# A three-block float32 model: convolution sums in two PSUM banks, and a recurrence in six levels with the next head's decay chain pulled forward

## The reference

```python
h = rmsnorm(concat(meta_tokens, x), norm_g)
glu_a, glu_b, z_conv, q, f, i, g_rec, m_conv, m_rec = split(h @ w_in)     # each 1024 wide
# convolution branch: 31 taps along the tokens, each channel by itself
a = glu_a * sigmoid(glu_b)
c = causal_conv(a, conv_w[31 taps]) + conv_b
y_conv = (silu(layernorm(c)) * silu(z_conv)) @ w_conv_out
# recurrence branch: 8 heads of 128 channels, in chunks
q = silu(q);  f = lb + (1 - lb) * sigmoid(f);  k = 1 - f;  v = i
b = cumsum(log f) within a chunk
o_intra[t] = sum_{s<=t} (sum_k q[t,k] k[s,k] exp(b[t,k] - b[s,k])) v[s]
o_inter[t] = (q[t] * exp(b[t])) @ S;   S = exp(b_last) * S + (k * exp(b_last - b))^T v
o = o_inter + o_intra, normalised per head, times silu(g_rec), then @ w_rec_out
out = x + (sigmoid(m_conv) * y_conv + sigmoid(m_rec) * y_rec) @ w_out
```

## Time and profile before

| | |
|---|---|
| median of 3 runs | 4041.17 us (4039.98 to 4044.63) |
| profiled execution | 4043.46 us, span of the trace 4041.8 us, so 1.7 us lie around it |
| mean granted TensorE clock | 0.965 |
| PE busy | 3775.2 us (93%) |
| DVE busy | 1746.9 us (43%) |
| ACT busy | 1139.4 us (28%) |
| POOL busy | 1018.8 us (25%) |
| chain that ended last | PE 76%, DVE 18%, ACT 3% |

### The profile page before, as it was taken

The page is one execution under the profiler, slowest core; times in us unless marked ns, Lnnn a source line. Parts: engine busy times, 40 slices in busy tenths (PEclk is TensorE's granted clock), DMA queues, the critical chain, the costliest instruction groups (busy, mean ns, idle before and its releaser), DMA issues.

```text
span 4041.8 us, 41623 instructions
## 1 busy us (share of the span) xinstructions
PE 3775.2 (93%) x17820; PEld 3089.0 (76%) x17820; DVE 1746.9 (43%) x1962; ACT 1139.4 (28%) x1412; POOL 1018.8 (25%) x408
## 2 busy tenths in 40 slices
PE   6999999998999989999989999998999979999996
PEld 6888887877778867666778888886777758888884
DVE  4565633999952344223332222224557152222225
ACT  4454432212141233443221111113322131111112
POOL 3343331222233431001322222222112332222221
PEclk9999999999999989999989999999999989999997
DMA  2000011111132221000211111112101201111111
GB/s 97 27 27 27 27 53 60 50 42 52 66 127 94 94 90 44 31 23 25 84 41 48 47 47 42 48 48 86 32 32 42 78 26 48 47 47 42 48 48 51
DMA packets 57927, 210.97 MB, mean 52 GB/s; under 512 B 6416, under 2 KB 6544, under 8 KB 57616
## 3 DMA queue, kind: packets, MB, share of 16 engines
q1 hardware_dynamic: 57744, 208.31, 15.4%
HBM read 183.12 MB, written 25.17 MB: 52 GB/s over the span
## 4 chain that ended last, share of the span: by engine, by line
PE 76%; DVE 18%; ACT 3%; issue 2%; POOL 1%; DMA 1%; SPq 0%; DVEq 0%; ACTq 0%
PE psum L418 65%; DVE Cb L1767 8%; PE psum L499 3%; PE psum L737 2%; PE psum L723 1%; PE psum L472 1%; PE psum L457 1%; DVE hl L1607 1%; PE psum L759 1%; DVE fb L1701 0%; DVE B L2310 0%; DVE Cb L1762 0%; POOL hl L2375 0%; DVE k L2252 0%; DVE work L1712 0%
## 5 line engine op out<-in xcount | busy, mean ns | idle before, releaser
L2358 POOL TENSOR_TENSOR wl<-raw,wh 128x1024 fp32r<-128x1024 f32 x283 | 707.7, 2502 | 2538.2 <-ACT wh L979 2538.2
L418 PE MATMUL psum<-hh,wh 128*128 128x512 f32 (+2 forms) x3760 | 1173.2, 398 | 98.0 <-POOL wl L2358 41.7
L418 PE MATMUL psum<-hh,wl 128*128 128x512 f32 (+2 forms) x3760 | 1123.9, 385 | 0.0
L418 PE MATMUL psum<-hl,wh 128*128 128x512 f32 (+2 forms) x3760 | 1118.3, 383 | 0.0
L418 PEld LDWEIGHTS psum<-hh,wh 128*128 128x128 f32 x3760 | 679.9, 194 | 244.9 <-issue 89.9
L418 PEld LDWEIGHTS psum<-hh,wl 128*128 128x128 f32 x3760 | 708.3, 192 | 137.8
L418 PEld LDWEIGHTS psum<-hl,wh 128*128 128x128 f32 x3760 | 705.9, 192 | 135.0
L979 ACT ACTIVATE wh<-raw 128x1024 fp32r<-128x1024 f32 x283 | 298.4, 1054 | 834.0 <-PE psum L418 827.3
L1767 DVE SCALAR_TENSOR_TENSOR Cb<-av,vec,Cb 128x1024 f32<-128x1024 f32 x240 | 376.2, 1567 | 8.3
L2092 DVE TENSOR_TENSOR B<-B,psum 128x1024 f32<-128x1024 f32 x128 | 156.4, 1222 | 491.1 <-PE psum L418 491.1
L418 PE MATMUL psum<-hdh,wh 128*128 128x512 f32 x1024 | 324.0, 397 | 0.0
(11 more groups left out here) (362 smaller groups left out, 3050.4 us busy)
## 6 DMA issues: line engine op xcount, KB each, us to landing
raw<-in_wts SPq DMA_DIRECT2D x283, 512.0 KB, 3.5
keep_x<-B SPq DMA_DIRECT2D x16, 512.0 KB, 3.8
t<-keep_x SPq DMA_DIRECT2D x15, 512.0 KB, 3.2
X<-in_xin SPq DMA_DIRECT2D x8, 520.0 KB, 5.2
keep_sz<-tmp SPq DMA_DIRECT2D x8, 512.0 KB, 2.9
av<-keep_gr SPq DMA_DIRECT2D x8, 512.0 KB, 3.2
tmp<-keep_sz SPq DMA_DIRECT2D x8, 512.0 KB, 3.8
av<-keep_gc SPq DMA_DIRECT2D x8, 512.0 KB, 3.3
```

The costliest lines, as they stand in the source:

```text
L418: ins = pe.matmul(out, w, x[:, k, c0:c0 + width], start=first and n == 0, stop=final and n == 2)
L2358: gp.tensor_tensor(wl[:, s, :], raw[:, s, :], fp(wh[:, s, :]), SUB).then_inc(*c.lo.tick(i))
```

## The change

Two things are changed at once, both in the first block.

**Convolution.** The running sum of the taps is a PSUM tile, `taps`, on banks 6 and 7; only the last tap writes `Cb[:, m]`. So that these banks are free, the ring `aux` is cut to bank 5 for this stretch, and the second of the two `gn` spreads goes into `head`'s bank.

**Recurrence.** Levels of halves 64 to 4 stay. The two smallest (2 and 1) and the diagonal become one last level over blocks of four tokens, whose mask includes the diagonal; for it ACT takes two full-width exponentials, DVE multiplies `kb` and `qb` in place by them, and `level(LAST, kk, q)` uses these. So a head has six levels instead of eight. The chain gate, logarithm, scan, difference, exponential and "kd" product of head h+1 is issued inside head h's job, in a fifth slot of `work` called `decay`; so are the differences of its levels 0 to 3 and the multiplications of levels 0 and 1. Both banks of a level are now issued in one step, the two transposes of a kind too. For head 0 the chain is issued before the first job.

```diff
-HALVES = (64, 32, 16, 8, 4, 2, 1)
+HALVES = (64, 32, 16, 8, 4, 2)
+LAST = len(HALVES) - 1
...
-        work = sb("work", [P, 4, TM], F, s)
+        work = sb("work", [P, 5, TM], F, s)
...
+    decay = work[:, 4, :]
+    def lev(lv):
+        return work[:, lv % 4, 0:T]
+    taps = flat(psum[:, 6:8, :])
...
@@ tensor(), hgrn(h)
+            pe.wait_ge(*c.ev("v", h, 2))
+            turned_v(0)
+            turned_v(1)
+            yield
+            pe.wait_ge(*c.hg_dve("kd", h))
+            turned_k(0)
+            turned_k(1)
+            yield from pause(2)
+            level(0, lev(0), lev(0))
+            yield
...
+            level(2, lev(2), lev(2))
+            yield from pause(2)
+            state(1)
+            yield
+            level(3, lev(3), lev(3))
+            yield from pause(3)
+            level(4, lev(4), lev(4))
+            yield from pause(3)
+            level(LAST, kk, q)
+            yield from pause(3)
+            output(0)
+            yield
+            output(1)
...
@@ tensor(), convolution
+                pe.wait_ge(*c.cv_act("root", 1))
+                aux.only(psum[:, 5, :])
...
-                x = grab(aux, ("gn", m, j), c.cv_dve("og", m, j))
+                x = grab((aux, head)[j], ("gn", m, j), c.cv_dve("og", m, j))
...
@@ scalar(), hgrn(h)
+            hgrn_exps(h, 4)
+            yield from pause(2)
+            se.wait_ge(*c.hg_pool("d", h, LAST))
+            se.wait_ge(*c.hg_pe("A", h, 2, 1))
+            se.activation(lev(LAST + 1), lev(LAST), EXP, scale=-1.0).then_inc(*c.hg_act.tick("e-", h, LAST))
+            se.wait_ge(*c.hg_act("e-", h, LAST))
+            se.activation(lev(LAST), lev(LAST), EXP).then_inc(*c.hg_act.tick("e", h, LAST))
+            yield
+            if ahead:
+                hgrn_log(ahead)
+            yield from pause(2)
+            if ahead:
+                hgrn_decay(ahead)
+            yield
+            se.wait_ge(*c.hg_pe("A", h, 3, 1))
+            se.activation(lev(LAST + 2), bx, EXP).then_inc(*c.hg_act.tick("qe", h))
...
@@ vector(), hgrn(h)
+            keep(2)
+            if ahead:
+                hgrn_gate(ahead)
+            yield
+            hgrn_mults(h, 4)
+            yield
+            state(1)
+            if ahead:
+                hgrn_scan(ahead)
+            yield
+            keep(3)
+            if ahead:
+                hgrn_decay(ahead)
+            yield from pause(2)
+            if ahead:
+                hgrn_kd(ahead)
+            yield
+            keep(4)
+            ve.wait_ge(*c.hg_act("qe", h))
+            ve.tensor_tensor(qe, qe, q, MUL).then_inc(*c.hg_dve.tick("qe", h))
+            yield
+            ve.wait_ge(*c.hg_dve("qe", h))
+            ve.tensor_tensor(kx, kx, lev(LAST + 1), MUL)
+            ve.tensor_tensor(q, q, lev(LAST), MUL).then_inc(*c.hg_dve.tick("right", h, LAST))
+            yield from pause(2)
+            keep(LAST)
+            yield from pause(3)
+            if ahead:
+                hgrn_mults(ahead, 0)
...
@@ vector(), convolve(m)
-            ve.tensor_scalar(Cb[:, m, :], u[:, 0:T], V("conv_w", m), V("conv_b", m), MUL,
+            if m:
+                ve.wait_ge(*c.cv_dve("c", m - 1))
+            ve.tensor_scalar(taps, u[:, 0:T], V("conv_w", m), V("conv_b", m), MUL,
                              ADD).then_inc(*c.cv_dve.tick("tap", m, 0))
             for j in range(1, TAPS):
+                last = j == TAPS - 1
                 ve.wait_ge(*c.cv_dve("tap", m, j - 1))
-                ve.scalar_tensor_tensor(Cb[:, m, :], u[:, j:j + T], V("conv_w", 8 * j + m), Cb[:, m, :], MUL,
+                ve.scalar_tensor_tensor(Cb[:, m, :] if last else taps, u[:, j:j + T], V("conv_w", 8 * j + m), taps, MUL,
...
@@ gpsimd(), hgrn(h)
+            yield from pause(9)
+            if ahead:
+                gp.wait_ge(*c.hg_dve("scan", ahead))
+                gp.wait_ge(*c.hg_pe("A", h, 4, 1))
+                below(ahead, 0)
+            yield from pause(2)
+            if ahead:
+                gp.wait_ge(*c.hg_dve("right", h, LAST))
+                below(ahead, 1)
```

More of the change, by code:

```diff
@@ L493, in turned_v, with level @@
                 ins.then_inc(*c.hg_pe.tick("vT", h, g))
[L495 to L500, removed]
+            def level(lv, left, right):
+                pe.wait_ge(*c.hg_dve("right", h, lv))
+                for g in range(2):
+                    x = grab(aux, ("A", h, lv, g), c.hg_dve("A", h, lv, g))
+                    for n in range(4):
+                        cc = slice((4 * g + n) * 128, (4 * g + n + 1) * 128)
+                        ins = pe.matmul(x[:, n * 128:(n + 1) * 128], left[:, cc], right[:, cc], start=True, stop=True)
+                    ins.then_inc(*c.hg_pe.tick("A", h, lv, g))
             def turned_k(g):
@@ L515, in state, with output @@
                 ins.then_inc(*c.hg_pe.tick("S", h, g))
[L517 to L553, removed]
+            def output(g):
                 x = grab(aux, ("o", h, g), c.hg_act("o", h, g))
[L555 to L558, removed]
+                pe.wait_ge(*c.hg_dve("A", h, LAST, g))
                 for n in range(4):
@@ L1101, in hgrn @@
             yield
[L1102 to L1111, removed]
+            hgrn_exps(h, 4)
[11 more added lines that the diff above has]
+                hgrn_decay(ahead)
+            yield
+            se.wait_ge(*c.hg_pe("A", h, 3, 1))
+            se.activation(lev(LAST + 2), bx, EXP).then_inc(*c.hg_act.tick("qe", h))
+            yield from pause(5)
+            if ahead:
+                hgrn_exps(ahead, 0)
+            yield from pause(2)
             for g in range(2):
@@ new lines, in hgrn_kd, with hgrn_mults @@
+        def hgrn_kd(h):
+            ve.wait_ge(*c.hg_act("wd", h))
+            ve.tensor_tensor(decay, decay, kb[:, h % 2, :], MUL).then_inc(*c.hg_dve.tick("kd", h))
+        def hgrn_mults(h, lv):
+            ul, ur = half(lev(lv), HALVES[lv])
+            ve.wait_ge(*c.hg_act("e", h, lv))
+            ve.tensor_tensor(ul, ul, half(kb[:, h % 2, META:TM], HALVES[lv])[0], MUL)
+            ve.tensor_tensor(ur, ur, half(qb[:, h % 2, :], HALVES[lv])[1], MUL).then_inc(*c.hg_dve.tick("right", h, lv))
@@ new lines, in hgrn, with keep @@
+            qe = lev(LAST + 2)
+            ahead = h + 1 if h < 7 else None
+            def keep(lv):
+                m = masks[:, lv:lv + 1, :].to_broadcast([P, 4, 128])
+                for g in range(2):
+                    dst, src = chunks(Ab[:, g * 512:(g + 1) * 512], 4), chunks(aux.of("A", h, lv, g), 4)
+                    ve.wait_ge(*c.hg_pe("A", h, lv, g))
+                    if lv == 0:
+                        ve.tensor_tensor(dst, src, m, MUL).then_inc(*c.hg_dve.tick("A", h, lv, g))
+                    else:
+                        ve.wait_ge(*c.hg_dve("A", h, lv - 1, g))
+                        ve.copy_predicated(dst, m.bitcast(I32), src).then_inc(*c.hg_dve.tick("A", h, lv, g))
@@ L1689, in hgrn @@
[L1689 to L1698 removed]
+            yield from pause(4)
@@ new lines, in hgrn @@
+        def hgrn(h):
+            ahead = h + 1 if h < 7 else None
+            yield from pause(4)
+            gp.wait_ge(*c.hg_pe("A", h, 0, 1))
+            below(h, 4)
+            yield from pause(2)
+            gp.wait_ge(*c.hg_pe("A", h, 1, 1))
+            below(h, LAST)
+            yield from pause(9)
+            if ahead:
+                gp.wait_ge(*c.hg_dve("scan", ahead))
+                gp.wait_ge(*c.hg_pe("A", h, 4, 1))
+                below(ahead, 0)
+            yield from pause(2)
+            if ahead:
+                gp.wait_ge(*c.hg_dve("right", h, LAST))
+                below(ahead, 1)
+            yield from pause(3)
+            if ahead:
+                below(ahead, 2)
+            yield from pause(2)
+            if ahead:
+                gp.wait_ge(*c.hg_pe("o", h, 1))
+                below(ahead, 3)
@@ L2421, in gpsimd @@
         for h in range(8):
+            if h == 0:
+                split(HGRN + 3)
+                gp.wait_ge(*c.hg_dve("scan", 0))
+                for lv in range(4):
+                    below(0, lv)
             for n in range(3):
```

241 lines of the change are left out of this document (100 added, 141 removed).

## The result

The changed kernel takes 3968.44 us (median of 4 runs, 3966.78 to 3970.26) against 4040.57 (4 runs, 4039.64 to 4044.63): ratio 0.982, interval 0.9803 to 0.9837. The forecast was 3977, its range 3932 to 4006. The profiled execution has a span of 3967.0, 74.8 less than before.

The account below looks back on a forecast made before the run. PE, busy 93% of the span, was taken to lose time to waits, in the convolution through DVE's taps. Convolution 37, seven heads 19 and the last head 8.5 made 64.5: 4041.2 - 64.5 = 3977 us, range 3932 to 4006.

Parts of the forecast that it names:

- The convolution, 37 us: Convolution: 30.5 us between the spreads plus the last spread's wait of 5.07 and its slow clock of about 1.5.
- I expect it to stop meeting POOL: Convolution: a tap reading one SBUF and one PSUM tile is no longer stretched by POOL; 68 us of DVE time go.
- The cover: Convolution: PE's slack over DVE per channel group, 2 us (48.1 against 46); above 1.38 us a tap DVE bounds again.
- the sum by rows: Convolution taps: from profile rows, a PSUM source adds nothing; 1.29 us a tap, against the skill's 0.065 us more.
- The wait at the last level: Recurrence: PE waits about 5.5 us a head for L1774, between 1.6 and 7, behind a DVE chain of 22 us.
- the 4 to 7 that the prediction named as its sign: Recurrence: the profile after would show PE waiting for L1774 seven times, 4 to 7 us each, none at the transposes.
- The slow clock: Recurrence: PE's reduced clock behind the wait at the last level costs 2 us a head.
- PE's own work: Recurrence: PE's work a head without waits and slow clock falls from 55.5 to 51.8 us.
- issuing halves together saves a further 0.5: Recurrence, PE: 0.5 us a head saved beyond the 3.2 us of the two levels dropped.
- the handovers: Recurrence: twelve handovers take about 0.2 us off a head's gain, so 2.7 us is counted instead of 2.9.
- The rivals: Chain hidden 0.12, dearer PSUM tap 0.14, heads gain nothing 0.10, slower by PSUM taps 0.04, no measurable effect 0.04.
- rival 1: Recurrence: chain hidden, PE waits 1.6 us or less, no slow clock, heads 52.5 to 54, 3921 to 3932; chance 0.12.

Follow-up runs that it names:

- experiment 5: Changed kernel with the taps' running sum alternating between the PSUM banks and the SBUF result tile: 3976.51 us, ratio 0.9837.
- Experiment 3: Also `late_split`: changed kernel with POOL's split of one slab held back until the last level's last product (L1774) is done: 3940.72 us, ratio 0.9752.
- experiment 4: Changed kernel with the next head's scan, difference, "kd" behind the last level's products on DVE, `qe`'s exponential ahead of the next decay on ACT: 3929.82 us.

## Why the prediction was right, step by step

- **The convolution, 37 us: right, and shown.** 30.5 between the spreads and 6.5 behind them. The spreads come every 48.1, and the step "I expect it to stop meeting POOL" is shown by experiment 5. The price of a tap was 1.290 (taken 1.29), and 1.323 from tap to tap (27.78 us for 21 of them). The cover is 3.0 us a group (DVE's wait for the slab's evacuation), the forecast had 2.
- **The PSUM source.** Taps that read PSUM and write SBUF take 1.281; those of the kernel before, which read and write SBUF, 1.285 in the median. The 62 further cycles that the Trainium skill, "VectorE: DVE Perf Modes", section "The TRN2 errata", gives a PSUM source are not in these rows; the sum by rows was the right one. What experiment 5 shows agrees with the Trainium skill, "SBUF — State Buffer", section "Who interferes with whom": a DVE instruction with two SBUF inputs contends with a GpSimd instruction that reads SBUF, one with at most one SBUF input (outside the two-port modes) does not.
- **The wait at the last level: right in place and mechanism, 3.8 in place of 5.5.** The chain took 20.8 us (274.16 to 294.97), forecast 22: undisturbed 17.3 (forecast 18.0), POOL 3.5 (0.9 at the gate, 0.5 at `qe`, 2.15 at L1774; forecast 4). The gate and the last product met POOL as forecast. The difference `below(h+1, 0)` started beside "kd" as forecast, but "kd" kept its time (1.24) and `qe` behind it was the one stretched. PE had 17.1 us of its own (274.16 to 291.25), forecast 16.4. So the wait came out at 3.70 to 3.78, under the 4 to 7 that the prediction named as its sign. Experiment 3 shows the one cause, the collision, and experiment 4 against 3 the other, the place in DVE's order.
- **The slow clock: 2.1 us in six heads of seven, forecast 2.0.** After a wait of 3.70 the first head had its last level in 2.05 us, at full speed, and took 57.4; the other six took 59.5 in the mean behind nearly the same wait (3.77 or 3.78).
- **PE's own work: the term that was too low.** Taken 51.8, measured 57.39 - 3.70 - 0.66 = 53.0. One step is seen to fail: "issuing halves together saves a further 0.5". Sixteen products of a level take 1.70 (272.46 to 274.16), more than two halves of 0.81. The rest, some 0.7, is in what I took off the kernel before for its slow clock: its heads were 62.6 to 63.7 apart, so the loss differs from head to head and one head's 2.8 was too much for all. Behind head 1's wait, for instance, the clock is 0.50 only from 152.6 to 156.0 us, with 3.3 us of PE's work in it: 1.6 lost. Three heads lost 2.8, the other four 1.6 or 1.7, in the mean 2.1. PE's own work before was then 56.3 a head and not 55.5, and the 3.3 by which it fell is about what two levels cost (3.2).
- **What the moved chain itself gave: next to nothing as it stood.** Waits and slow clock together took 6.6 us a head before (62.9 less 56.3) and 6.2 after (59.2 less 53.0). So of the 25.8 us of the seven heads some 23 are the two levels that are gone. This split is worked out from the traces; no run has the levels or the moved chain alone. Experiment 4 shows what the chain was worth in another place: 38.6 us more, of which 27.7 come already when the collision alone goes (experiment 3).
- **The sum.** A head took 59.2 where 60.0 stood (60.2 with the handovers), 6.8 us less for seven; the last job took 9.4 less (12.1 less the 2.7 that come behind it) where 8.5 stood; with the 0.6 ahead of the heads, 3.6 in stages that the change does not touch, and 1.6 given back to the clock behind the heads, that is the 10.3 us by which the span shrank more than forecast (74.8 for 64.5). The medians differ from the forecast by 8.6. That a head came so close is in part luck: PE's own work was 1.2 us more than taken and the wait 1.7 less, and the two errors, 8 and 12 us over seven heads, cancel for the most part.
- **The rivals.** None of the five occurred. Experiment 3 makes the kernel much like rival 1 (waits of 1.6 us, no slow clock), yet its heads are 55.3 apart and not 52.5 to 54, since PE's own work is 53.0 and not 51.8, and it takes 3941 where rival 1 has 3921 to 3932. Experiment 4 reaches 3930 by another order of DVE's row, which moves the products out of the split's way and the chain out of theirs.

## What to carry to other kernels

A wait that vanishes is looked for again one place further on: here 28.2 us left the transposes and 26.5 came back at the last level, because a chain that nobody needed yet stood in an in-order queue ahead of one that was needed next. Order such a queue by who is waited for first. And where POOL runs beside a long running sum, try the sum in PSUM, so that DVE reads only one of its large inputs from SBUF: here POOL then cost the taps nothing.

## What the hardware showed that was not expected

- Where DVE and POOL meet, the one that comes second waits: L1774 and `qe` end 1.08 us behind the POOL instruction they met, and so do all 33 stretched taps of the kernel before (1.08 to 1.09). So what a meeting costs goes by how much of the other's instruction is still to run. A product of half the width does the same in the earlier trace rows: it ends at 217.67, POOL at 217.13, 0.54 earlier.
- The gate's first pass reads one large SBUF tile only and is stretched all the same (1.72 against 0.82 us). So it is not a count of inputs alone that decides; what sets the gate apart from a tap that reads PSUM is not shown by a run here, but it is the quicker one, 1040 elements in 0.82 us against 1024 in 1.28.
- A DVE tap that writes PSUM costs hardly more than one that writes SBUF (1.290 against 1.281 us, both with a PSUM source).
- The slow clock is not in step with the wait: 3.70 us without it in one head, 3.77 with it in the others; 3.5 us brought it in every head of the kernel before, and 1.6 us, in `late_split`, in none of seven.
